# Last two y units taken by halves of the frames, and the next unit's first 128 weight columns prepared ahead, at the three norm boundaries of a streaming encoder step

## The reference, cut to what matters

```python
def rms_norm(x, g):
    return x * rsqrt(mean(x * x, -1) + 1e-6) * g

h = rms_norm(x, pre_mix_g[l])
y = even_mixer(h, ...) if l % 2 == 0 else gla_mixer(h, ...)   # ends in  @ w_out
x = x + rms_norm(y, post_mix_g[l])                            # boundary 0 (l = 0), boundary 2 (l = 1)
h = rms_norm(x, pre_ffn_g[l])
y = (silu(h @ w_gate) * (h @ w_up)) @ w_down                  # D_FF = 2816
x = x + rms_norm(y, post_ffn_g[l])                            # boundary 1 (l = 0)
```

## Time and profile before

| | |
|---|---|
| runs | 1441.9, 1445.85, 1445.97 us |
| profiled execution | 1442.83 us, span 1440.3 us, mean granted clock of TensorE 0.989 |
| TensorE busy | 1381.8 us (96% of the span) |
| VectorE, ScalarE, GpSimd busy | 822.6, 530.2, 390.2 us |
| bytes read and written in HBM | 114.42 and 15.74 MB, 90 GB/s over the span |
| boundary 0, 1, 2 | about 160 to 212, 615 to 675, 955 to 1008 us from the span's start |

### The profile page before, as it was taken

How to read it: one execution, slowest core, us unless ns; L and a number is a source line. 1 busy time by engine, 2 the same in 40 slices (tenths; PEclk the granted TensorE clock), 3 DMA queues, 4 the chain that set the end, 5 groups by cost and what they waited for, 6 DMA issues and landing times.

```text
span 1440.3 us, 20834 instructions
## 1 busy us (share of the span) xinstructions
PE 1381.8 (96%) x9097; PEld 1312.1 (91%) x9097; DVE 822.6 (57%) x928; ACT 530.2 (37%) x741; POOL 390.2 (27%) x307
## 2 busy tenths in 40 slices
PE   7999989999999999988999999998999999999996
PEld 7999979999999999977899877997979898999996
DVE  5256576765655556476433454647686565555744
ACT  6132252542424334333333223324245243433444
POOL 2241153333333243123001100005243333324304
PEclk9999999999999999989999999999999999999998
DMA  7221122122221222314141321421312222222231
GB/s 242 90 67 66 59 99 92 59 89 88 88 89 59 89 88 75 142 56 156 36 145 60 123 82 59 161 74 57 134 59 88 88 68 95 73 88 88 89 118 73
DMA packets 92072, 131.49 MB, mean 91 GB/s; under 512 B 2559, under 2 KB 76107, under 8 KB 91214
## 3 DMA queue, kind: packets, MB, share of 16 engines
q1 hardware_dynamic: 87328, 108.64, 22.8%
q0 software_dynamic: 3808, 19.42, 3.8%
q10 hardware_dynamic: 846, 2.11, 0.4%
HBM read 114.42 MB, written 15.74 MB: 90 GB/s over the span
## 4 chain that ended last, share of the span: by engine, by line
PE 77%; DVE 14%; ACT 4%; issue 3%; POOL 2%; ACTq 0%; DMA 0%; DVEq 0%; SPq 0%; POOLq 0%
PE ps L553 25%; PE ps L544 19%; PE ps L634 5%; PE ps L589 5%; PE ps L1057 4%; PE ps L801 4%; PE ps L786 4%; PE ps L744 4%; DVE wl L1118 2%; DVE wl L1253 1%; PE ps L1030 1%; POOL x L2124 1%; PE ps L1043 1%; DVE up L1320 1%; PE ps L686 1%
## 5 line engine op out<-in xcount | busy, mean ns | idle before, releaser
L1118 DVE TENSOR_TENSOR wl<-stage,wh 128x2048 fp32r<-128x2048 f32 x57 | 139.7, 2452 | 79.8 <-ACT wh L1745 44.4
L1736 ACT ACTIVATE wh<-stage 128x2048 fp32r<-128x2048 f32 x47 | 89.7, 1908 | 183.0 <-PE ps L544 122.9
L2195 POOL TENSOR_TENSOR wsum<-stage 128x512 f32<-128x512 f32 x36 | 46.7, 1296 | 401.5 <-DVE wl L1253 249.8
L1253 DVE TENSOR_TENSOR wl<-wsum,wh 128x2048 fp32r<-128x2048 f32 x36 | 82.5, 2291 | 30.0 <-ACT wh L1765 29.8
L544 PE MATMUL ps<-xh,wh 128*128 128x320 f32 x352 | 81.8, 314 | 3.9 <-DVE qk L1124 2.4
L1814 ACT ACTIVATE gate<-ps 128x320 f32<-128x320 f32 x72 | 31.3, 434 | 143.0 <-PE ps L553 143.0
L1246 DVE TENSOR_TENSOR wbl<-stage,wbh 128x1024 fp32r<-128x1024 f32 x36 | 44.4, 1233 | 66.9 <-ACT wbh L1755 66.9
L544 PE MATMUL ps<-xl,wh 128*128 128x320 f32 x352 | 81.5, 313 | 0.0
L544 PE MATMUL ps<-xh,wl 128*128 128x320 f32 x352 | 81.3, 313 | 0.0
L589 PE MATMUL ps<-wh,xh 128*128 128x256 f32 x240 | 68.1, 284 | 0.0
L589 PE MATMUL ps<-wh,xl 128*128 128x256 f32 x240 | 67.9, 283 | 0.0
(11 more groups left out here) (366 smaller groups left out, 4473.1 us busy)
## 6 DMA issues: line engine op xcount, KB each, us to landing
stage<-w_ffn_gate SPq DMA_DIRECT2D x22, 1024.0 KB, 5.4
stage<-w_ffn_up SPq DMA_DIRECT2D x22, 1024.0 KB, 5.3
stage<-w_ffn_down SPq DMA_DIRECT2D x22, 1024.0 KB, 5.1
stage<-w_in_odd SPq DMA_DIRECT2D x12, 1024.0 KB, 5.3
x_spill<-x POOLq DMA_DIRECT2D x3, 2560.0 KB, 8.5
x<-x_spill SPq DMA_DIRECT2D x3, 2560.0 KB, 10.6
stage<-w_in_even SPq DMA_DIRECT2D x6, 1024.0 KB, 5.1
stage<-w_out_even SPq DMA_DIRECT2D x4, 1024.0 KB, 5.1
```

The costliest lines, as they stand in the source:

```text
L1118: dve.tensor_tensor(wl[:, s].rearrange("p k c -> p (k c)"), stage[:, s, :], f32(wh[:, s].rearrange("p k c -> p (k c)")), ALU.subtract).the ...
L1253: dve.tensor_tensor(wsl[:, u % 2, :], wsum[:].rearrange("p i c -> p (i c)"), f32(wsh[:, u % 2, :]), ALU.subtract).then_inc(w_lo, 1)
L1736: act.activation(wsh[:, u % 2, :], flat_stage(u), ACT.Copy).then_inc(w_hi, 1)
```

## The change

- Units three and four of y (here a and b) are taken together, in this order of quarter parts: a m0 h0, a m1 h0, b m0 h0, b m1 h0, a m0 h1, sum of half 0, a m1 h1, spread of half 0, b m0 h1, b m1 h1 (`last_y_units`). VectorE copies and ScalarE squares the first five parts one by one; `y_out` of unit three as a whole is gone. VectorE and ScalarE handle a m1 h1, b m0 h1 and b m1 h1 in and among the boundary's first pieces.
- The PSUM banks of the half sums and half spreads move to the banks of b.
- The boundary's first unit u: in boundaries 0 and 2, `hi(u)` comes after the five squares and `lo(u)` after the scaling of piece 1 (they were inside the third y unit). In boundary 1 they stay among the y units.
- The second unit (u + 1): its first 128 columns are made high after piece 4 (`hi_ahead`) and low after piece 5 (`lo_ahead`), each over 128x1024 values. The other 128 columns (boundaries 0 and 2 only) follow after the last piece on ScalarE, and on VectorE after the pre-norm's diagonal matrix. `hi(u + 1)` after piece 3 and `lo(u + 1)` after piece 9 are gone.
- The new x's squares: ScalarE keeps four pieces behind instead of three, and VectorE makes all of their sums, 2x1280 three times instead of twice; GpSimd's sum (L2128) is gone.
- The half 1 norm: GpSimd's power comes after piece 5 instead of 4, `half_diag` after piece 7 instead of 6. TensorE's sum stays after piece 1 and waits for the last square sums of half 1, which VectorE makes after piece 4.

```diff
-            return (own + 1, other + 2), (own + 3, other + 3), other + 2, other + 3
+            return (other + 2, other + 3), (other, other + 1), other + 2, other + 3
# TensorE
-            def last_y_unit(u, B, mh, ml, nk, wv=None, place=None):
...
-                for m, h in ((0, 0), (1, 0), (0, 1)):
-                    part(wv, out, mh, ml, m, h, range(nk), nk, place).then_inc(y_blocks_full, 1)
-                pe.wait_ge(acc_empty, g)
-                sum_half(B, 0)
-                now = min(nk - 1, 6)
-                last = part(wv, out, mh, ml, 1, 1, range(now), nk, place)
...
-                spread_half(B, 0)
-                    part(wv, out, mh, ml, 1, 1, range(now, nk), nk, place).then_inc(w_used, 1)
+            def last_y_units(ua, ub, B, mh, ml, nk, wvs=None, place=None):
+                g = B["g"] - 2
+                wva, wvb = wvs or (views(ua), views(ub))
+                a_out, b_out = banks4(g), banks4(g + 1)
+                pe.wait_ge(w_lo, ua + 1)
+                pe.wait_ge(acc_empty, g - 1)
+                for m in range(2):
+                    part(wva, a_out, mh, ml, m, 0, range(nk), nk, place).then_inc(y_blocks_full, 1)
+                pe.wait_ge(w_lo, ub + 1)
+                pe.wait_ge(acc_empty, g)
+                for m in range(2):
+                    part(wvb, b_out, mh, ml, m, 0, range(nk), nk, place).then_inc(y_blocks_full, 1)
+                part(wva, a_out, mh, ml, 0, 1, range(nk), nk, place).then_inc(y_blocks_full, 1)
+                sum_half(B, 0)
+                part(wva, a_out, mh, ml, 1, 1, range(nk), nk, place).then_inc(w_used, 1)
+                spread_half(B, 0)
+                part(wvb, b_out, mh, ml, 0, 1, range(nk), nk, place).then_inc(y_blocks_full, 1)
+                part(wvb, b_out, mh, ml, 1, 1, range(nk), nk, place).then_inc(w_used, 1)
# VectorE, y units
+                y_stand(B, add, 3, 1, 0, 0)
+                add_square(B, 1, 0, 0)
+                add_square(B, 2, 1, 0)
+                y_stand(B, add, 4, 1, 1, 0)
+                add_square(B, 3, 0, 0)
+                if n == 1:
+                    lo(ahead[2])
+                y_stand(B, add, 5, 0, 0, 1)
                 half_ms(B, 0)
+                add_square(B, 5, 0, 1)
                 half_diag(B, 0)
+                dve.wait_ge(w_used, ends[2])
+                y_piece(B, add, 0, 1, 1).then_inc(acc_empty, 1)
# VectorE, boundary, after the scaling of piece i
-                    if i == 0:
-                        dve.wait_ge(w_used, used(u - 1))
-                        last_piece(B, add, 1, 1).then_inc(acc_empty, 1)
                     if i >= LAG:
                         x_lo(B, i - LAG)
-                    if i == 4:
+                    if i == 1 and n != 1:
+                        lo(u)
+                    elif i == 2:
+                        y_stand(B, add, 6, 1, 0, 1)
+                        add_square(B, 6, 1, 1)
+                    elif i == 3:
+                        dve.wait_ge(w_used, used(u - 1))
+                        y_piece(B, add, 1, 1, 1).then_inc(acc_empty, 1)
+                    elif i == 4:
+                        add_square(B, 7, 0, 1)
+                    elif i == 5:
+                        lo_ahead(B)
                         half_ms(B, 1)
-                    elif i == 6:
+                    elif i == 7:
                         half_diag(B, 1)
-                    elif i == 9:
-                        lo(u + 1)
...
+                for i, squared in enumerate((12, 14, 16)):
+                    dve.wait_ge(x_squares, PIECES * n + squared)
+                    if i:
+                        dve.wait_ge(x_squares_added, 4 * n + i)
+                    dve.tensor_tensor(acc[:], acc[:] if i else y[:, 0:2], y[:, 2 * i + 2:2 * i + 4], ALU.add).then_inc(x_squares_added, 1)
...
+                if n != 1:
+                    dve.wait_ge(w_hi, u + 2)
+                    dve.tensor_tensor(wl[:, (u + 1) % 2, :, P:], blocks_of(u + 1, 1), f32(wh[:, (u + 1) % 2, :, P:]), ALU.subtract).then_inc(w_lo, 1)
# ScalarE, boundary, after xh of piece i
                     if i == 0:
-                        act.wait_ge(acc_empty, B["g"])
-                        square_piece(1, 1)
-                    elif i == 3:
-                        hi(u + 1)
-                    target = i - 3 if i < 12 else 2 * i - 15 if i < PIECES - 1 else PIECES
+                        act.wait_ge(acc_empty, B["g"] - 1)
+                        square_piece(B, 0, 1, 1, 1)
+                    elif i == 2:
+                        act.wait_ge(y_stands, 6 * n + 6)
+                        square_piece(B, 1, 0, 1, 6)
+                    elif i == 3:
+                        act.wait_ge(acc_empty, B["g"])
+                        square_piece(B, 1, 1, 1, 7)
+                    elif i == 4:
+                        hi_ahead(B)
+                    target = i - 4 if i < 12 else 2 * i - 15 if i < PIECES - 1 else PIECES
# GpSimd
-                    if i == 4:
+                    if i == 5:
                         norm_half(B, 1)
-                pool.wait_ge(x_squares, PIECES * n + 12)
-                pool.tensor_tensor(acc[:], y[:, 0:2], y[:, 2:4], ALU.add).then_inc(x_squares_first, 1)
```

More of the change, by code:

```diff
@@ L343, in encoder, with ahead_of, blocks_of, wait_ahead @@
         BOUNDS = (
-            dict(n=0, gp=POST_MIX, gq=PRE_FFN, g=G_FF0, x=X_FF0),
-            dict(n=1, gp=POST_FFN, gq=PRE_MIX + 8, g=G_QK, x=X_IN1),
-            dict(n=2, gp=POST_MIX + 8, gq=PRE_FFN + 8, g=G_FF1, x=X_FF1),
-        )
+            dict(n=0, gp=POST_MIX, gq=PRE_FFN, g=G_FF0, x=X_FF0, u=U_FF0),
+            dict(n=1, gp=POST_FFN, gq=PRE_MIX + 8, g=G_QK, x=X_IN1, u=U_QK),
+            dict(n=2, gp=POST_MIX + 8, gq=PRE_FFN + 8, g=G_FF1, x=X_FF1, u=U_FF1),
+        )
+        def ahead_of(B, t):
+            v = B["u"] + 1
+            src = stage[:, v % 2, 0:KB * P].rearrange("p (k c) -> p k c", c=P) if B["n"] == 1 else blocks_of(v, 0)
+            return t[:, v % 2, :, 0:P], src
+        def blocks_of(u, m):
+            return stage[:, u % 2, :].rearrange("p (k c) -> p k c", c=UW)[:, :, m * P:(m + 1) * P]
+        def wait_ahead(engine, B, own, whole):
+            if B["n"] == 1:
+                engine.wait_ge(whole, B["u"] + 2)
+            else:
+                engine.wait_ge(own, B["n"] // 2 + 1)
         def f32(t):
@@ L927, in mixed @@
                     pe.wait_ge(yb_lo, TT)
-            for m in range(3):
+            for m in range(2):
                 if m == 1:
```

105 lines of the change are left out of this document (54 added, 51 removed).

## The result

The changed kernel takes 1421.96 us, median of 5 (1421.56 to 1423.28), where the kernel before took 1445.9 (1441.9 to 1446.54) on the same chip: ratio 0.984, 95% interval 0.9827 to 0.9854. The profiled execution took 1421.9 us with a span of 1419.9. The gain is 23.9 us where 14.8 to 15.9 was forecast; the time lies under the range (1424 to 1438.5).

What follows compares the result with a forecast made beforehand. In boundaries TensorE was taken to wait for VectorE's `x_lo`. Gains of 3.8, 3.8 and 7.2 sum to 14.8 us (8 to 18 from the bounds); from 1442.83, 1428.0, with most of a 3.0 difference back 1430.0; range 1424 to 1438.5.

Steps and rivals of the forecast that it cites:

- the pace's 0.15: Boundaries 0 and 2: of the 4.3 us gained at the last `x_lo`, TensorE loses some 0.15 to the last pieces' pace.
- The head start: Boundaries 0 and 2: the reordered y parts let VectorE scale piece 0 at 964.55 instead of 970.84, 6.3 us sooner.
- the signs of being wrong: VectorE waits over 2.5 us for squares, a TensorE wait for `wl`, clock under 0.8 over a boundary, y parts over 3.52.
- More, less and added waits on VectorE: Boundaries 0 and 2, before the last `x_lo`: 8.2 us more (3.5 of it waits), 6.2 less; it comes 4.3 sooner.
- The lock: VectorE's `lo(u)` holds GpSimd's add of piece 1 some 2 us; the half 1 sum moves by 0.4 at most.
- TensorE on this schedule: TensorE held 1.7 us up to the half 1 sum, 1.1 at piece 4's low part, 1.0 at the spread; no cost.
- After piece 15: Boundary's end: VectorE's longer sums take 5.3 us, so TensorE now waits 0.3 us.
- Boundary 1: First scaling 7.0 us sooner, last `x_lo` 7.6, last low pass 7.5; less 0.3, a gain of 7.2 us.
- What else moves: Load of unit u + 3, freed some 16 us later in boundaries 0 and 2: nothing if covered, else up to 2 us each.
- Rival 2: More comes back: shorter gaps leave the clock at 1.00 everywhere and waits at their lower bound; 21 us, 1424, chance 0.13.
- the head start was not eaten: Against rival 1: VectorE-ScalarE hand-overs among the first five pieces cost 7 us, not 3.5; gain 4.3, 1440.5, chance 0.15.
- rival 3: Gaps from the half 1 sum on keep TensorE's clock low to piece 15, 8.3 us a boundary; 1455, chance 0.05.

Runs made afterwards that it cites:

- the first pair: First profiles of the kernel before and of the changed kernel, nothing further edited; median times 1445.9 and 1421.96 us.
- the repeats: Both kernels profiled and timed again, nothing edited: kernel before 1445.04 us; changed kernel 1422.67 and 1421.98 us.

## Why the prediction was wrong

The mechanism held; the size did not. The table takes all profiles of the two unedited kernels (2 and 3), with the idle time of TensorE apart from its busy time. Where a stage is paced by TensorE, a longer busy time of the same products is a lower clock. Inside a boundary the two trade against each other, so there the split says where TensorE's time went and not what the clock cost.

| stage | before | after | gained | of it idle | of it busy | forecast |
|---|---|---|---|---|---|---|
| boundary 0 | 88.02 | 83.46 | 4.6 | 4.2 | 0.4 | 3.8 |
| boundary 1 | 60.51 | 51.58 | 8.9 | 3.8 | 5.1 | 7.2 |
| stage behind it | 56.89 | 55.58 | 1.3 | 0 | 1.3 | 0 |
| boundary 2 | 96.58 | 90.91 | 5.7 | 3.5 | 2.2 | 3.8 |
| stage behind it | 58.56 | 57.44 | 1.1 | 0.8 | 0.3 | 0 |
| sum | | | 21.6 | 12.3 | 9.3 | 14.8 |

Cut at VectorE's first scaling and at the end of its last `x_lo`, the boundaries show where the size was off. The scaling comes 6.2, 7.0 and 6.2 us sooner in the first pair (6.3, 7.0 and 6.3 forecast; over the repeats boundary 1 has 7.3). The part behind the last `x_lo` is 0.5 us longer in each (the 0.3 and the pace's 0.15 of the prediction). The stretch between them changed by +0.75, -1.0 and +1.65 us in the first pair and by +1.1, -2.3 and -0.1 over the repeats, where +2.0, -0.6 and +2.0 was forecast. All that the boundaries gave beyond the forecast lies in that stretch: 2.0 us in the first pair, 4.7 over the repeats.

- **The head start**: right to 0.15 us (23.50 against 23.35). Of the signs that the prediction named, three came: in boundary 2 the scaling of piece 0 (949.40) begins 7.0 us before the first L690 product (956.43), the last `x_lo` takes 0.55 us, and no gap ahead of piece 9 is over 2 us. The lengths were right for boundaries 1 and 2 in the first pair (7.57 and 4.04); boundary 0 gained 4.93, more than the 3 to 4.5 named. None of the signs of being wrong came.
- **More, less and added waits on VectorE**: net right in boundary 2 of the first pair (4.5 sooner, 4.3 forecast), item by item wrong. The square sum after piece 2 needs the square that ScalarE makes after piece 0, not the one after piece 2: I counted the semaphore one too high. The 1.5 and 0.5 us don't exist. In their place stand the copy's 0.33, `lo_ahead`'s 0.30 (0.5 forecast), the spread's 1.22 (1.0) and 0.95 us by which two square sums last longer: 2.8 for my 3.5. The run with the waits put in says that this error was worth 1.65 us of the time, over three boundaries.
- **The lock**: `lo(u)` held GpSimd's add as forecast. ScalarE's `xh` of piece 1 then stood 2.47 us for that add, but VectorE and TensorE came for its result later still. What I left out is that VectorE's own short sums meet GpSimd's adds too.
- **TensorE on this schedule**: holds 0.86, 0.42 and 1.42 us where I had 1.7, 1.1 and 1.0. Inside the head start, as forecast.
- **After piece 15**: TensorE waits 0.20 for the sum, 0.3 forecast.
- **Boundary 1**: 7.57 in the first pair against 7.2, 8.9 over the repeats.
- **What else moves**: the load of u + 3 has cover, as forecast.
- **The failed step is the clock.** I wrote of the clock of 0.55 behind 675.2 "I leave as it is", and of the 3.0 us between the profiled execution and the median that most of it comes back. Both took the low clock of the kernel before for a constant. Time off full clock fell from 21.0 us (64 runs) to 12.4 (15 runs). In the first pair it shows as the 3.08 us of the stage behind boundary 1 and as a profiled execution that is no longer faster than its median (1421.9 and 1421.96). In the repeats it shows inside boundary 2, where low clock on the half 1 sum and spread cost the kernel before 3.45 us in one of its two profiles; the three of the changed kernel lie within 1.0 us (90.81, 91.44, 90.47). What the 8.6 us are worth in all can only be estimated: at the 0.47 us each that the runs of the kernel before show, 4.1 of the 8 us missed. The 15 runs of the changed kernel show 0.14 each, with a weak correlation (0.37), and by that it would be 1.2. In boundary 1 low clock stands beside the excess too (0.89 before, 0.93 to 0.97 after), but no run shows how much of it that is. Rival 2 named this step and gave it 1424 and a chance of 0.13; it was the nearest.
- **The other rivals**: the head start was not eaten, and the clock was 0.93 to 0.98 over the boundaries with low stretches of 5 to 15 us, so rival 3's low clock to piece 15 didn't come.
- **The bounds**: waits at 2 instead of 3.5 us, three times, make the gain 19.3 by the prediction's own figures, not the 18 that it gives; the fast end of the range came from rival 2 in any case.
- **A term at nothing** is the 1.1 us behind boundary 2, in a stage whose instructions the change doesn't edit; I hadn't foreseen it. The section on the hardware has it. With the first pair: 1.7 us in the boundaries, 3.1 behind boundary 1, 1.1 behind boundary 2, 2.0 between profile and median, 7.9 in all.

What stays open: whether the low clock behind boundary 1 depends on the change. That stage is 54.6 us at full clock. In seven profiles of kernels without the whole change it was 57.65, 56.12, 55.76, 57.55, 54.58, 56.11 and 56.13; in nine with it 54.57, 54.58, 54.58, 54.58, 54.57, 54.58, 56.12, 57.48 and 57.59. One of seven and six of nine at full clock is a tendency, not more; the gap ahead of the half sum, which I held to be its cause, is not. That the kernel as a whole spends less time off full clock after the change is shown by its runs. Where in the kernel each part of the change does that is not shown.

## What to carry over

Profile the kernel before more than once, and split each stage into TensorE's idle time and the busy time of the same products. In the stages that TensorE paces, the idle time repeated to the hundredth (2.82 us), and the busy time moved with the granted clock by 1.5 us steps; inside the changed kernel's boundaries idle time moved too, by up to 1.8 us. This change, which removed idle time in several places, took low clock with it, so a part of the range belonged on the fast side (here an estimated 1 to 4 us on top of 15). A wait put on VectorE cost less than its length, since other waits shrank by it (0.4 to 1.3 of 1.74 us). One put on TensorE ahead of the half 0 sum, on which the first scaling hangs, cost about all of it (2.4 over the mean, for a gap of 2.3, where the profiles behind that mean lie 2.2 apart).
